# Row products that finish bank by bank, norms by token half, and an output in quarters, in a three-block network on one core

## The reference

```python
x = layer_norm(DN_ALPHA * x + mix, ln_g[l, 0], ln_b[l, 0])
x = layer_norm(DN_ALPHA * x + peer_ffn(x, ...), ln_g[l, 1], ln_b[l, 1])
...
x = x + 0.5 * swiglu(rms_norm(x, ffn1_norm[l]), ...)
h = rms_norm(x, mix_norm[l])
x = x + (gate_a * y_a + gate_b * y_b) @ w_out[l]
x = x + 0.5 * swiglu(rms_norm(x, ffn2_norm[l]), ...)
return rms_norm(x, final_norm)
```

## Time and profile before

| | |
|---|---|
| three runs, median (lowest to highest) | 2911.38 us (2909.59 to 2913.31) |
| profiled execution, its own time | 2910.83 us |
| its span, first to last instruction | 2908.9 us |
| mean granted TensorE clock | 0.965 of full speed |
| TensorE busy | 2757.5 us, 95% of the span |
| VectorE / ScalarE / GpSimd busy | 1875.2 / 1262.7 / 719.9 us |
| the chain that ended last | 85% TensorE, 11% VectorE |

### The profile page before, as it was taken

One profiled execution on the slowest core, in us unless ns is written; L12 is line 12 of the kernel. 1 busy time (PEld: TensorE's weight loads), 2 busy tenths in 40 slices (PEclk: granted clock), 3 DMA queues, 4 the chain that ended last, 5 costly groups with the idle time before them and its releaser, 6 DMA issues.

```text
span 2908.9 us, 43684 instructions
## 1 busy us (share of the span) xinstructions
PE 2757.5 (95%) x17592; PEld 2498.6 (86%) x17592; DVE 1875.2 (64%) x3241; ACT 1262.7 (43%) x1761; POOL 719.9 (25%) x312
## 2 busy tenths in 40 slices
PE   8998999999999989789999999999889999998998
PEld 7878999999888867579999997888789788897896
DVE  5655997777555566658987775555555586435554
ACT  4433554333454535434553334454444463322443
POOL 0000887666000001007986660000000101000000
PEclk9999999999999999899999999999999999977999
DMA  5554554444666654344554446666545552112454
GB/s 198 169 192 138 176 180 146 144 139 148 193 191 192 191 164 125 99 151 157 179 163 143 140 138 200 190 193 191 181 143 179 172 160 73 37 52 95 159 183 144
DMA packets 123977, 451.52 MB, mean 155 GB/s; under 512 B 13809, under 2 KB 13937, under 8 KB 123649
## 3 DMA queue, kind: packets, MB, share of 16 engines
q1 hardware_dynamic: 121952, 441.57, 47.5%
q0 software_dynamic: 1824, 7.17, 0.7%
HBM read 446.59 MB, written 2.10 MB: 154 GB/s over the span
## 4 chain that ended last, share of the span: by engine, by line
PE 85%; DVE 11%; ACT 1%; POOL 1%; issue 1%; DMA 0%; DVEq 0%; SPq 0%; ACTq 0%
PE ps L497 11%; PE ps L447 11%; PE ps L448 11%; PE ps L449 11%; PE ps L498 11%; PE ps L499 11%; DVE W L1359 8%; PE ps L568 4%; PE ps L469 3%; PE ps L471 3%; PE ps L470 3%; PE ps L696 3%; DVE x L1359 1%; POOL lo L2064 1%; PE ps L433 1%
## 5 line engine op out<-in xcount | busy, mean ns | idle before, releaser
L939 ACT ACTIVATE hi<-ring 128x1024 fp32r<-128x1024 f32 x830 | 878.4, 1059 | 1193.5 <-PE ps L449 644.4
L1382 DVE TENSOR_TENSOR lo<-ring,hi 128x1024 fp32r<-128x1024 f32 x564 | 689.9, 1225 | 596.2 <-ACT hi L939 596.0
L447 PE MATMUL ps<-xT_r,hi 128*128 128x256 f32 x3248 | 935.7, 288 | 11.7 <-POOL lo L2064 8.1
L448 PE MATMUL ps<-xT_r,hi 128*128 128x256 f32 x3248 | 920.7, 283 | 0.0
L449 PE MATMUL ps<-xT_r,lo 128*128 128x256 f32 x3248 | 920.4, 283 | 0.0
L2064 POOL TENSOR_TENSOR lo<-ring,hi 128x1024 fp32r<-128x1024 f32 x266 | 674.6, 2543 | 556.6 <-ACT hi L939 556.6
L447 PEld LDWEIGHTS ps<-xT_r,hi 128*128 128x128 f32 x3248 | 624.9, 192 | 15.6 <-POOL lo L2064 5.5
L448 PEld LDWEIGHTS ps<-xT_r,hi 128*128 128x128 f32 x3248 | 625.4, 193 | 0.8 <-issue 0.7
L449 PEld LDWEIGHTS ps<-xT_r,lo 128*128 128x128 f32 x3248 | 624.8, 192 | 0.0
L497 PE MATMUL ps<-hi,oht_r 128*128 128x512 f32 x1040 | 410.3, 394 | 11.6 <-DVE x L1359 7.0
L498 PE MATMUL ps<-lo,oht_r 128*128 128x512 f32 x1040 | 407.7, 392 | 0.0
(11 more groups left out here) (218 smaller groups left out, 2873.8 us busy)
## 6 DMA issues: line engine op xcount, KB each, us to landing
ring<-in_peer_u SPq DMA_DIRECT2D x256, 512.0 KB, 3.5
ring<-in_peer_v SPq DMA_DIRECT2D x256, 512.0 KB, 4.2
ring<-in_f SPq DMA_DIRECT2D x132, 512.0 KB, 3.5
ring<-in_ret_vg SPq DMA_DIRECT2D x32, 512.0 KB, 3.5
ring<-in_peer_q SPq DMA_DIRECT2D x32, 512.0 KB, 3.6
ring<-in_ret_qk SPq DMA_DIRECT2D x16, 512.0 KB, 4.5
ring<-in_ret_out SPq DMA_DIRECT2D x16, 512.0 KB, 3.8
ring<-in_in_shift SPq DMA_DIRECT2D x14, 512.0 KB, 3.9
```

The costliest lines, as they stand in the source:

```text
L447: pe.matmul(o, h, xT[:, k, 0:256], start=k == 0, stop=False)
L448: pe.matmul(o, h, xT[:, k, 256:512], start=False, stop=False)
L939: hid.done(a.activation(hi[m % NH][:, :], ring[j % NR][:, :], ACT.Copy), j)
L1382: lo_v.done(v.tensor_tensor(lo[m % NH][:, :], ring[j % NR][:, :], as32(hi[m % NH][:, :]), ALU.subtract), j)
```

## The change

1. `mat_out_steps` treats the last two tiles of a row product bank by bank: for each bank first the three matmuls of the last but one tile, then the three of the last. Each bank gets an event of its own, `(name, "out", q)`. (The one use with `fine=True`, inside the mixer, keeps the old order.)
2. `layer_norm` waits for each bank by itself, makes the variance of each token half by itself, and finishes half 0 before half 1. The mean-square norm is split in the same way (`mean_square`, `scaled`). GpSimd takes the inverse root in two 1-element steps (`roots`).
3. The first tile of the next sub-layer gets its `lo` from GpSimd, and VectorE makes the second tile's `lo` after the norm in place of before it. ACT copies that tile's `hi` after its squares in two of the joints.
4. The transposes wait for the part that they read: (half 1, first column half) for the first ones, then the rest.
5. At the end S_xs is gone: one instruction does scale and gain per quarter of 128 x 512; four transfers of 256 KB write the output, each when its quarter is ready; the load of the gain row waits for feed-forward 2's last hidden product, no longer for its last addition to x.

```diff
-                add("peer_q", l * 16 + i)
+            add("peer_q", l * 16 + i, "V" if i else "P")
...
+                last = len(tiles) - (0 if fine else 2)
...
+                for k in range(last):
+                    awaited(k)
+                    for q in range(4):
+                        ins = quarter(k, q)
...
+                if not fine:
+                    for q in range(4):
+                        for k in (last, last + 1):
+                            if q == 0:
+                                awaited(k)
+                            ins = quarter(k, q)
+                            if q == 3 and k == last:
+                                mm.done(ins, "eaten", tiles[k])
+                        mm.done(ins, name, "out", q)
+                    mm.also("eaten", tiles[-1])
                 mm.also(name, "out")
...
-                pe.wait_ge(*at(dve, "norm", l, 0))
-                parts(("peer", l), lambda tt, c: tok3(x, tt, c), 8)
+                parts(("peer", l), lambda tt, c: tok3(x, tt, c), 8, ready=lambda c: at(dve, "norm", l, 0, 3 if c else 2))
...
-            def layer_norm(src, l, i):
-                v.wait_ge(*at(mm, src, "out"))
+            def layer_norm(src, l, i, between=None):
+
                 for tt in range(2):
                     for nh in range(2):
                         xv = x[:, tt, nh * 512:nh * 512 + 512]
+                        v.wait_ge(*at(mm, src, "out", tt * 2 + nh))
                         stt_(xv, xv, ALPHA, ps(src, tt * 2 + nh), ALU.mult, ALU.add)
                         empties(dve, src, tt * 2 + nh)
                         step(v.bn_stats, rs_st[:, tt, nh, :], xv)
                     step(v.bn_aggr, rs_mv[:, tt, :], rs_st[:, tt, :, :].rearrange("p h s -> p (h s)"))
-                ts_(rs_r, rs_mv[:, :, 1], 1.0, LN_EPS, ALU.mult, ALU.add, name=("var", "ln", l, i))
+                    ts_(rs_r[:, tt:tt + 1], rs_mv[:, tt, 1:2], 1.0, LN_EPS, ALU.mult, ALU.add, name=("var", "ln", l, i, tt))
                 v.wait_ge(*loaded(("gb", l, i)))
                 for tt in range(2):
                     stt_(x[:, tt, :], x[:, tt, :], rs_mv[:, tt, 0:1], gbt[:, 0:1024], ALU.subtract, ALU.mult)
-                v.wait_ge(*at(pool, "rsqrt", "ln", l, i))
-                for tt in range(2):
+                    if tt and between is not None:
+                        between()
+                    v.wait_ge(*at(pool, "rsqrt", "ln", l, i, tt))
                     for half in range(2):
...
+            def mean_square(stage, tt):
+                v.wait_ge(*at(act, "squares", stage, tt))
+                tt_(rs_s[:, tt:tt + 1], rs_q[:, tt, 0:1], rs_q[:, tt, 1:2], ALU.add)
+                ts_(rs_r[:, tt:tt + 1], rs_s[:, tt:tt + 1], 1.0 / DM, RMS_EPS, ALU.mult, ALU.add, name=("var", "rms", stage, tt))
+
+            def scaled(stage, xs, tt):
+                v.wait_ge(*at(pool, "rsqrt", "rms", stage, tt))
+                for half in range(2):
+                    ts_(xs[:, tt, half * 512:half * 512 + 512], x[:, tt, half * 512:half * 512 + 512], rs_r[:, tt:tt + 1], None,
+                        ALU.mult, name=("rms", stage, tt, half))
+
+            def rms(stage, xs, added):
+
+                for k in range(3):
+                    added(k)
+                mean_square(stage, 0)
+                added(3)
+                scaled(stage, xs, 0)
+                mean_square(stage, 1)
+                scaled(stage, xs, 1)
...
-                for i in range(16):
+                for i in range(15):
                     split(TILE["ret_out", i] + 2)
...
                 layer_norm("ret_out", 0, 0)
+                split(TILE["peer_q", 1])
...
+            for k in range(3):
+                ffn_added(2)(k)
+            mean_square("last", 0)
+            ffn_added(2)(3)
             v.wait_ge(*loaded("final"))
             for tt in range(2):
-                tt_(x[:, tt, :], S_xs[:, tt, :], gbt[:, 0:1024], ALU.mult, name=("final",))
+                v.wait_ge(*at(pool, "rsqrt", "rms", "last", tt))
+                for half in range(2):
+                    xv, gv = x[:, tt, half * 512:half * 512 + 512], gbt[:, half * 512:half * 512 + 512]
+                    stt_(xv, xv, rs_r[:, tt:tt + 1], gv, ALU.mult, ALU.mult, name=("final", tt, half))
+                if tt == 0:
+                    mean_square("last", 1)
...
-            load("final", [(gbt[:, 0:1024], prow(8, 1024))], [at(dve, "ffn", 2)])
-            power(rs_r, "rms", "last")
+            roots("rms", ("ffn", 2))
+            load("final", [(gbt[:, 0:1024], prow(8, 1024))], [at(mm, "ffn", 2, 21)])
+            roots("rms", "last")
...
-            sp.wait_ge(*at(dve, "final"))
-            sp.dma_start(out.rearrange("(a p) d -> p a d", p=128), x).then_inc(s_out, 16)
-            sp.wait_ge(s_out, 16)
+            for quarter in range(4):
+                sp.wait_ge(*at(dve, "final", quarter // 2, quarter % 2))
+                sp.dma_start(*aside(quarter)).then_inc(s_out, 16)
+            sp.wait_ge(s_out, 64)
```

More of the change, by code:

```diff
@@ L426, in bank, with parts @@
                 return psum[b]
-            def parts(stage, src, nchunk, among=tuple(range(8)), first=0):
+            def parts(stage, src, nchunk, among=tuple(range(8)), first=0, ready=None):
                 for c in range(first, nchunk, 2):
                     b = bank(stage, "T", c, among=among)
+                    if ready is not None:
+                        pe.wait_ge(*ready(c))
                     for j in range(2):
@@ L483, in mat_out_steps, with awaited @@
                 bs = [bank(name, k, among=among) for k in range(4)]
-                for k, i in enumerate(tiles):
+                last = len(tiles) - (0 if fine else 2)
+                def awaited(k):
                     if ahead is not None:
                         ahead(k)
-                    v = lhs(k)
-                    n = NTH[i] % NH
-                    pe.wait_ge(*low(i))
+                    pe.wait_ge(*low(tiles[k]))
                     for w in ready(k):
                         pe.wait_ge(*w)
-                    for tt in range(2):
-                        ah, al = v[:, tt * 128:tt * 128 + 128], v[:, 256 + tt * 128:256 + tt * 128 + 128]
-                        for nh in range(2):
-                            b = bs[tt * 2 + nh]
-                            h, l = hi[n][:, nh * 512:nh * 512 + 512], lo[n][:, nh * 512:nh * 512 + 512]
-                            pe.matmul(b, ah, h, start=k == 0, stop=False)
-                            pe.matmul(b, ah, l, start=False, stop=False)
-                            ins = pe.matmul(b, al, h, start=False, stop=k == len(tiles) - 1)
-                            if fine and tt * 2 + nh < 3:
-                                yield
-                    mm.done(ins, "eaten", i)
@@ new lines, in quarter @@
+                def quarter(k, q):
+                    v, n = lhs(k), NTH[tiles[k]] % NH
+                    tt, nh = q // 2, q % 2
+                    ah, al = v[:, tt * 128:tt * 128 + 128], v[:, 256 + tt * 128:256 + tt * 128 + 128]
+                    h, l = hi[n][:, nh * 512:nh * 512 + 512], lo[n][:, nh * 512:nh * 512 + 512]
+                    pe.matmul(bs[q], ah, h, start=k == 0, stop=False)
+                    pe.matmul(bs[q], ah, l, start=False, stop=False)
+                    return pe.matmul(bs[q], al, h, start=False, stop=k == len(tiles) - 1)
@@ L1142, in ffn @@
                 cut(21)
-                for i in range(22):
+                for i in range(21):
                     split(TILE[f"f{n}_2", i] + 2)
@@ L1338, in mixer @@
                 parts("mixT", 8, M_mT)
-                for i in range(8):
+                for i in range(7):
                     split(TILE["w_out", i] + 2)
@@ L1588, in peer @@
                 weigh(126)
-                for k in range(128):
+                for k in range(127):
                     if k < 126:
@@ L1592, in peer @@
                     split(TILE["peer_v", l * 128 + k] + 2)
-                layer_norm(("peer_v", l), l, 1)
+                if l == 0:
+                    layer_norm(("peer_v", l), l, 1)
+                    split(TILE["diff_q", 1])
+                else:
+                    layer_norm(("peer_v", l), l, 1, between=lambda: mean_square(("ffn", 1), 0))
+                    scaled(("ffn", 1), F_xs, 0)
+                    mean_square(("ffn", 1), 1)
+                    scaled(("ffn", 1), F_xs, 1)
             def softmax_in(name, pt, s, kw, mask, mx):
@@ L2072, in power, with roots @@
                           "rsqrt", *name)
+            def roots(*name):
+                for tt in range(2):
+                    power(rs_r[:, tt:tt + 1], *name, tt)
             def peer(l):
@@ L2077, in peer @@
                 gains(l, 1, mm, "peer_u", l, 126)
-                power(rs_r, "ln", l, 1)
+                split(TILE["peer_v", l * 128 + 127] + 1)
+                roots("ln", l, 1)
             n = CONW["ident"]
@@ L2086, in gpsimd_program @@
```

(3 more changed lines are left out.)

82 lines of the change are left out of this document (42 added, 40 removed).

## The result

The changed kernel takes 2889.86 us (median of 4, 2888.72 to 2890.81) against 2912.35 of before (4 runs, 2909.59 to 2916.77): ratio 0.9921, 95% interval 0.9904 to 0.9938. It is faster by 22.5 us, not by the 30.3 forecast, and lies above the range. The profiled execution took 2890.81, its span 2889.0, so 19.9 less than the span of 2908.9 before.

A forecast was written before the change was run, and what follows sets the result against it. TensorE was taken to bound the kernel (85% of the chain), its matmul stream unchanged. Joints' gains of 14.4 + 4.6 + 6.3 and the end's 5.0 made 30.3 us off 2910.83: 2880.5, stated as 2881, range 2877.5 to 2887.5.

The forecast's parts named there:

- Joints: TensorE's waits between sub-layers: 4.8 us shorter at three layer-norm joints, 4.6 at one with both norms, 3.15 at two mean-square ones.
- The end: From last matmul to the span's end: 8.85 us in place of 13.8, a gain of 5.0 (3.9 to 6.3).
- the landing of the last quarter: Last 256 KB output transfer at the kernel's end: lands in 3.2 us, bounds 1.8 and 4.3.
- The moves: First next tile's subtraction to GpSimd (2.41 us), second (1.23) behind the norm: both covered, no stall in the last pair.
- Most of the time is the stream of matmuls, which this change leaves as it is.: TensorE's matmuls, most of the 85% of the chain on that engine: same instructions and tiles, so no time gained or lost.
- The rival of a clock that outlasts the transposes: Two short joints: slow clock ends no earlier than now, losing 3.2 us together, giving 2884; chance 0.07.
- My slower rival: Stream after every joint: clock stays low, 36 us lost at 12 us per spell beyond the transposes, giving 2917; chance 0.02.
- the port rival: Joints: VectorE is held while GpSimd subtracts, up to 2.4 us in each of four, about 10, giving 2891; chance 0.06.

The follow-up runs named there:

- old_order: Changed kernel with the last two tiles of every row product back in the old matmul order, all else kept: 2902.47 us, ratio 0.9972.
- v_first: Changed kernel with VectorE, not GpSimd, making the low part of the next sub-layer's first tile at all six joints: 2889.87 us, ratio 0.9932.
- before_again: The kernel before, no edit, profiled and timed once more: 2910.21 us, ratio 1.0002.
- delay_small: Changed kernel plus one needless VectorE addition of 128 x 256 at the joint from feed-forward 1 to the mixer: 2878.61 us, ratio 0.988.
- delay_two: Changed kernel plus two needless VectorE additions of 128 x 1024 at the joint from feed-forward 1 to the mixer: 2887.83 us, ratio 0.9919.
- fox_split: Changed kernel with the first head's small score matmuls in the mixer issued ahead of the round's dense weight tile: 2875.05 us, ratio 0.9884.
- fox_before: Kernel before with the first head's small score matmuls in the mixer issued ahead of the round's dense weight tile: 2926.05 us, ratio 1.0033.

## Why the prediction was wrong, point by point

**Joints.** The mechanism was right: without the new order of matmuls on TensorE the norm by halves brings nothing (old_order). The size was a little off: 4.4 in place of 4.8 three times, 3.9 in place of 4.6, 2.9 in place of 3.15 twice; 2.4 us in all. I chained durations taken from instructions that follow each other on VectorE. Where one waits for another engine's event, some 0.07 to 0.1 more pass: 215.38 + 0.69 to the addition at 216.18, 0.11, against 0.03 from 211.18 + 0.69 to 211.90. The layer-norm chain has several such places, and from the first addition to the first transpose it took 12.2 us, where I had 11.9. That these places make up the whole of it is an estimate.

**The end.** 6.2 in place of 5.0. VectorE's part was right (5.1 for 5.2); the term that was mis-sized is the landing of the last quarter, taken as 3.2 and measured as 2.0. I had put it between a row of 4.3 and one of 1.8. The 4.3 rows belonged to transfers queued behind 512 KB loads, and the last quarter has only its sister ahead, 0.8 us earlier. The Trainium skill, DMA: Bandwidth & Descriptors, gave about 2.5 by my estimate from its fixed cost of 2.0 us and was nearer than my choice.

**The moves.** No stall inside the last pair of tiles, GpSimd's split at 2.40, second split covered: as forecast. Moving the first split off VectorE is worth 0.9 in each of four joints (v_first), which I had not priced apart.

**The step that failed.** "Most of the time is the stream of matmuls, which this change leaves as it is." The instructions stay, their pace does not. I put this term at nothing without a reason, and it measured 10.4 lost in the mixer. I looked for the clock behind the joints only, and misread it there: it comes back 2.8 to 4.1 us behind the first transpose in the trace of before, not 3.2 everywhere. In the changed kernel it comes back 1.9 later behind two joints, 0.8 later behind one and 0.3 to 0.9 earlier behind three. The rival of a clock that outlasts the transposes was priced at 3.2 for the two short joints and cost some 1.3, behind two others. My slower rival wanted low clock in the stream after *every* joint and found nothing for it in the windows; it looked for the right cost in the wrong place. The windows over the mixer, 0.96 and 0.70 in the trace of before, would have shown that the clock had work to lose there; the spells behind the groups of scores, that it does so in fits of some microseconds. A change that shifts these stretches by 3 us can then cost or give 10. Sum by the traces: 29.2 won in joints and end, 4.6 in the first expert layer, 10.4 lost in the mixer, 3.5 in pieces: 19.9. That the measured 2889.86 lies next to the port rival's 2891 is an accident; nothing of that rival is in the trace.

The 4.6 are for the most part the same term with the other sign. In that layer low clock fell from 10.2 us (6.8 in before_again, where it took 1.4 less) to 3.4, and half of 6.8 is 3.4. It is not the change's merit alone: delay_small, delay_two, fox_split and v_first, with the changed kernel's program up to there but for v_first's splits, have no low clock in it and took 1.5 less than the changed kernel.

In the kernel before and the changed one the mixer's spells ahead of its last third repeat to 0.1 us between two profiles of each; the five runs of delay_two lie 10 us apart, those of fox_before 30. The Trainium skill, TensorE: Matmul & The Clock Gate, in What's actually happening, says of the slow matmuls at a kernel's start that their number varies from run to run with where the gate stands then, and that their penalty, under 1% of a typical kernel's span, is not to be fitted. The scatter of delay_two and fox_before looks like the first, the two kernels compared do not show it. The page speaks of the start, not of a stream under way; there the mixer's loss of 10.4 us is 0.4% of the time, but half of what the change brought.

**Still open.** Why the executions of before agree with each other and those of delay_two do not; why a group of scores is followed by low clock in one place and not in another; what makes the other 1.2 us of the 4.6 in the first expert layer; what makes the 58 us spell vanish in fox_split.

## What to carry to other kernels

A sum over the edited places gives what the edit is worth, and it was good to 4% here (29.2 for 30.3, two errors of opposite sign in it); beside it stands a term of either sign for stretches of light matmuls that run at a mixed clock: a third of the gain here (10.4), and 25 us between two kernels that differ in 2.6 us of needless work. Price it from the windows of before: a stretch at 0.96 and one at 0.70 have room in both directions, and the range must hold it. Judge such an edit by its own stretch in the trace and not by the total, count the low clock in that stretch, and before calling an edit of the matmuls' order good, run it again with half a microsecond of needless work ahead of it.

## What the runs showed of the hardware

- Half a microsecond of useless VectorE work ahead of a mixer of 371 us made it 11 us shorter, and in the profiled executions 2.6 us turned another order of its matmuls from 353.1 into 378.4.
- Low clock in that mixer cost half its length: 85.3 to 116.1 us of it in eleven traces, and 315.1 to 317.3 us left when half is taken off.
- Low clock came in a stream in which TensorE was busy by 98% (117.4 of 120 us), in or right behind groups of twelve matmuls on 64 and 8 rows, four of eight groups in one kernel and seven of eight in the other.
- A 256 KB transfer with nothing but its like in the queue landed in 2.0 us, where 1 MB had taken 4.0.
- VectorE additions with one input in PSUM (0.69) and GpSimd's subtraction (2.40) do not slow each other.
